# A two-layer hybrid trunk: later parameter loads and identity turns at the start, another order at the norm boundaries, in memory attention and in its projections

## What is computed

```python
for i in range(2):
    mem_kv = rmsnorm(mem, mem_norm[i]) @ w_mem_kv[i]              # keys and values of the memory
    proj = rmsnorm(h, norm_mix_pre[i]) @ w_in[i]
    y_mix = ssd_mixer(proj) if i == 0 else window_attention(proj)  # Mamba-2 SSD / 16 heads, window 128, sinks
    y_mem = memory_cross_attention(proj, mem_kv)                   # 4 heads of 128, softmax over 256 tokens
    h = h + rmsnorm(concat(y_mix, y_mem) @ w_out[i], norm_mix_post[i])
    f = square(relu(rmsnorm(h, norm_mlp_pre[i]) @ w_up[i])) @ w_down[i]   # 1024 -> 4096 -> 1024
    h = h + rmsnorm(f, norm_mlp_post[i])
```

## Time and profile before

| | us |
|---|---|
| median of 3 runs | 1384.0 (1383.21 to 1384.0) |
| profiled execution, own time | 1384.49 |
| its span, first to last instruction | 1382.4 |
| mean granted TensorE clock | 0.997 |
| TensorE busy with products and turns | 1346.0 (97%) |
| VectorE busy | 688.1 (50%) |
| ScalarE busy | 585.6 (42%) |
| GpSimd (POOL) busy | 121.3 (9%) |
| memory read | 133.44 MB, 99 GB/s over the span |

### The profile page before, as it was taken

How to read it: one execution, slowest core, us unless ns; L and a number is a source line. 1 busy time by engine, 2 the same in 40 slices (tenths; PEclk the granted TensorE clock), 3 DMA queues, 4 the chain that set the end, 5 groups by cost and what they waited for, 6 DMA issues and landing times.

```text
span 1382.4 us, 17791 instructions
## 1 busy us (share of the span) xinstructions
PE 1346.0 (97%) x6631; PEld 1114.8 (81%) x6631; DVE 688.1 (50%) x1070; ACT 585.6 (42%) x1103; POOL 121.3 (9%) x131
## 2 busy tenths in 40 slices
PE   6999999999999999999999999999999999999998
PEld 5788888888778888888888888776788888888886
DVE  5566686787435544223443454775364432244333
ACT  5555355566434443223432333664344432234321
POOL 0045252651000000000000000000000000000000
PEclk9999999999999999999999999999999999999999
DMA  6253433243422323242232133112223322322322
GB/s 205 72 144 94 118 100 113 99 147 105 164 92 63 110 87 107 97 133 91 91 107 92 62 99 111 47 62 77 70 67 98 97 96 99 114 92 92 106 92 77
DMA packets 75645, 137.73 MB, mean 100 GB/s; under 512 B 6391, under 2 KB 16951, under 8 KB 75575
## 3 DMA queue, kind: packets, MB, share of 16 engines
q1 hardware_dynamic: 71184, 134.76, 30.2%
q10 hardware_dynamic: 4390, 2.02, 0.8%
HBM read 133.44 MB, written 2.93 MB: 99 GB/s over the span
## 4 chain that ended last, share of the span: by engine, by line
PE 85%; DVE 8%; ACT 3%; issue 2%; DMA 1%; POOL 1%; ACTq 0%; DVEq 0%; SPq 0%; POOLq 0%
PE G L1656 56%; PE X L1656 12%; PE X L1679 5%; PE X L1727 3%; DVE conv L1209 2%; DVE wlo L1080 1%; PE X L1907 1%; PE X L1835 1%; PE X L2090 1%; PE G L1727 1%; ACT whi L555 1%; PE X L1826 1%; DMA raw<-in_w_up 1%; DVE ulo L1408 1%; PE X L2117 1%
## 5 line engine op out<-in xcount | busy, mean ns | idle before, releaser
L1080 DVE TENSOR_TENSOR wlo<-raw,whi 128x1024 fp32r<-128x1024 f32 x224 | 275.0, 1233 | 452.5 <-ACT whi L555 451.6
L555 ACT ACTIVATE whi<-raw 128x1024 fp32r<-128x1024 f32 x224 | 235.5, 1058 | 438.8 <-PE G L1656 234.0
L1656 PE MATMUL G<-uhi,whi 128*128 128x512 f32 x736 | 294.3, 400 | 3.1 <-DVE ulo L1097 1.8
L1656 PE MATMUL G<-uhi,wlo 128*128 128x512 f32 x736 | 287.1, 390 | 0.0
L1656 PE MATMUL G<-ulo,whi 128*128 128x512 f32 x736 | 286.6, 389 | 0.0
L1656 PEld LDWEIGHTS G<-uhi,whi 128*128 128x128 f32 x736 | 138.3, 188 | 33.2 <-issue 3.2
L1656 PEld LDWEIGHTS G<-uhi,wlo 128*128 128x128 f32 x736 | 138.1, 188 | 29.6
L1656 PEld LDWEIGHTS G<-ulo,whi 128*128 128x128 f32 x736 | 138.4, 188 | 28.4
L1656 PE MATMUL G<-whi,hidhi 128*128 128x512 f32 x256 | 99.6, 389 | 0.0
L1656 PE MATMUL G<-whi,hidlo 128*128 128x512 f32 x256 | 99.6, 389 | 0.0
L1656 PE MATMUL G<-wlo,hidhi 128*128 128x512 f32 x256 | 99.6, 389 | 0.0
(11 more groups left out here) (328 smaller groups left out, 2255.1 us busy)
## 6 DMA issues: line engine op xcount, KB each, us to landing
raw<-in_w_up SPq DMA_DIRECT2D x64, 512.0 KB, 3.8
raw<-in_w_down SPq DMA_DIRECT2D x64, 512.0 KB, 3.5
raw<-in_ssd_w_in SPq DMA_DIRECT2D x20, 512.0 KB, 3.6
raw<-in_w_mem_kv SPq DMA_DIRECT2D x16, 512.0 KB, 3.5
raw<-in_ssd_w_out SPq DMA_DIRECT2D x16, 512.0 KB, 3.5
raw<-in_swa_w_in SPq DMA_DIRECT2D x16, 512.0 KB, 3.8
raw<-in_ssd_w_in SPq DMA_DIRECT2D x16, 384.0 KB, 3.3
csrow<-cs_rows SPq DMA_DIRECT2D x16, 384.0 KB, 4.5
```

The lines of the kernel that those rows point to most:

```text
L555: act.activation(whi[q][:, :, :], raw[q % 2][:, :, :], ACT.Copy).then_inc(hi_done, 1)
L1080: dve.tensor_tensor(wlo[q][:, :, :], raw[q % 2][:, :, :], whi[q][:, :, :].bitcast(F32), ALU.subtract).then_inc(lo_done, 1)
L1656: mm = pe.matmul(o, st, mv, start=(kt == 0 and fresh and not go_on), stop=(q == total - 1 and k == 1), skip_group_check=True)
```

## The change

The rest of the code is as it was. Three of the eight parameter loads are gone, since nothing reads those rows of `par` (the gains come a second time through `g_post` and `g_pre`); `par` is filled accordingly (44 columns in place of 92).

```diff
+WARM = 20
-MEM_AT = {32 + 8 * i + r: (i, r) for i in range(2) for r in range(4)}
+MEM_AT = {29 + 11 * i + r: (i, r) for i in range(2) for r in range(4)}
-        g_gate = par[:, 80:92]
+        g_gate = par[:, 32:44]
@@ scalar: parameter loads
-            rows = (("mem_norm", 0, 16), ("norm_mix_pre", 16, 16), ("norm_mix_post", 32, 16),
-                    ("norm_mlp_pre", 48, 16), ("norm_mlp_post", 64, 16), ("ssd_gate_norm", 80, 12))
-            for name, r0, n in rows:
-                act.dma_start(par_rows[r0:r0 + n, 0, :],
+            for j, name in enumerate(("mem_norm", "norm_mix_pre")):
+                act.dma_start(par_rows[16 * j:16 * j + 16, 0, :],
                               a[name].rearrange("i (k p) -> (i k) p", p=P)).then_inc(par_in, 16)
-            act.dma_start(par_rows[0:80, 1, :],
-                          a["ssd_conv_w"][0].rearrange("w (k p) -> (w k) p", p=P)).then_inc(par_in, 16)
-            act.dma_start(par_rows[80:100, 1, :],
-                          a["ssd_conv_b"].rearrange("i (k p) -> (i k) p", p=P)).then_inc(par_in, 16)
...
             act.activation(eps[:, 4:5], eps[:, 0:1], ACT.Sqrt)
+            act.dma_start(par_rows[32:44, 0, :],
+                          a["ssd_gate_norm"].rearrange("i (k p) -> (i k) p", p=P)).then_inc(par_in, 16)
+            act.dma_start(par_rows[0:80, 1, :],
+                          a["ssd_conv_w"][0].rearrange("w (k p) -> (w k) p", p=P)).then_inc(par_in, 16)
+            act.dma_start(par_rows[80:100, 1, :],
+                          a["ssd_conv_b"].rearrange("i (k p) -> (i k) p", p=P)).then_inc(par_in, 16)
             for t in range(NT):
                 act.wait_ge(x_in[t], 16)
                 token_rms(t, x_tok[:, t, :], xn[:, t, :])
@@ scalar: mem_copy(i, j, part), part 0 banks 0 and 1 (or values of tile 0), part 1 the rest
                 if next_panel is not None:
+                    i, j = divmod(p // 4 - B_MEM, 2)
+                    if p % 4 == 3:
+                        mem_copy(i, j, 0)
                     ahead(*next_panel)
+                    if p % 4 == 3:
+                        mem_copy(i, j, 1)
...
-                else:
-                    mem_copy((blk - B_MEM) // 2, (blk - B_MEM) % 2)
@@ scalar: boundary
                 hi(nb, 1)
-                hi(nb, 2)
                 norm_out(m, 3)
                 norm_in(m, 2)
+                hi(nb, 2)
+                norm_in(m, 3)
                 hi(nb, 3)
-                norm_in(m, 3)
                 u_hi(m, 2)
                 u_hi(m, 3)
@@ vector: start
-            dve.wait_ge(par_tr, 2)
-            dve.tensor_copy(par[:, 0:92], X[3][:, 0:92]).then_inc(par_done, 1)
-            dve.tensor_scalar(par[:, 92:192], X[3][:, 128:228], 0.5, None, ALU.mult).then_inc(par_done, 1)
             for t in range(NT):
                 token_norm(t, x_tok[:, t, :], xn[:, t, :])
+                if t == 1:
+                    dve.wait_ge(par_tr, 2)
+                    dve.tensor_copy(par[:, 0:44], X[3][:, 3 * P:3 * P + 44]).then_inc(par_done, 1)
+                    dve.tensor_scalar(par[:, 92:192], X[2][:, 3 * P:3 * P + 100], 0.5, None,
+                                      ALU.mult).then_inc(par_done, 1)
@@ vector: memory_step
-                if tp == 0 and h >= 1:
+                if tp == 1 and h >= 1:
                     memory_lo(i, yh, yl, B, h - 1)
@@ vector: boundary
                 add_out(m, 3)
+                lo(nb, 2)
                 scaled(m, 2)
-                lo(nb, 2)
+                lo(nb, 3)
                 scaled(m, 3)
-                lo(nb, 3)
@@ vector: attention_panel
                         w_norm(u)
+                        if slot in Q_OUT:
+                            queries(N_QB, B_QB, 1, 2 * Q_OUT[slot])
                         if todo is not None:
                             ahead(*todo)
                             todo = None
...
-                    if slot in Q_OUT:
-                        queries(N_QB, B_QB, 1, 2 * Q_OUT[slot])
@@ tensor: split
-                            elif half == 0 and (q, b) == (3, 1):
+                            elif half == 0 and (q, b) == (3, 0):
                                 turn_u(m, 3, f)
@@ tensor: start
             pe.wait_ge(consts, 1)
-            pe.wait_ge(par_in, 128)
-            pe.transpose(X[3][:, 0:92], par_rows[0:92, 0, :], ident[0:92, 0:92]).then_inc(par_tr, 1)
-            pe.transpose(X[3][:, 128:228], par_rows[0:100, 1, :], ident[0:100, 0:100]).then_inc(par_tr, 1)
+            for x in range(WARM):
+                pe.transpose(G[0][:, 0:P], ident[:, :], ident[:, :])
             for t in range(NT):
+                if t == 1:
+                    pe.wait_ge(par_in, 80)
+                    pe.transpose(X[3][:, 3 * P:3 * P + 44], par_rows[0:44, 0, :], ident[0:44, 0:44]).then_inc(par_tr, 1)
+                    pe.transpose(X[2][:, 3 * P:3 * P + 100], par_rows[0:100, 1, :],
+                                 ident[0:100, 0:100]).then_inc(par_tr, 1)
                 pe.wait_ge(tok_norm, t + 1)
                 for k in range(KT):
-                    if t == 0 and k == KT - 1:
+                    if t == 1 and k == KT - 2:
                         pe.wait_ge(par_done, 2)
```

More of the change, by code:

```diff
@@ L580, in mem_hi, with mem_copy @@
                                    scale=g_mem[i][:, 2 * r + x:2 * r + x + 1]).then_inc(uhi_ready, 1)
-            def mem_copy(i, j):
+            def mem_copy(i, j, part):
                 n = 2 * i + j
                 if j == 0:
-                    for b in range(4):
+                    for b in (2 * part, 2 * part + 1):
                         group_ready(act, N_MEM + n, 4 * (B_MEM + n) + 4, b)
@@ L588, in mem_copy @@
                 else:
[L589 to L593, removed]
+                    t = part
+                    group_ready(act, N_MEM + n, 4 * (B_MEM + n) + 4, 2 * t + 1)
+                    for x in range(2):
+                        act.activation(memV[i][:, t, M * x:M * x + M], G[t][:, M * x:M * x + M],
+                                       ACT.Copy).then_inc(bank_free[t if x else 2 + t], 1)
             act.wait_ge(eps_done, 1)
             act.activation(eps[:, 4:5], eps[:, 0:1], ACT.Sqrt)
+            act.dma_start(par_rows[32:44, 0, :],
[4 more added lines that the diff above has]
+                          a["ssd_conv_b"].rearrange("i (k p) -> (i k) p", p=P)).then_inc(par_in, 16)
             for t in range(NT):
```

## The result

The changed kernel takes 1359.95 us (median of 6 runs, 1359.74 to 1360.34), the kernel before beside it 1383.08 (6 runs, 1381.85 to 1384.0): a ratio of 0.9833, with a 95% interval of 0.982 to 0.9845. The forecast was 1363.0. It had the sign right, and the mechanisms but for part of the start, and was 3 us too high; the result lies just under the low end of the range, 1360.0. The profiled execution took 1359.76 us (span 1357.7; before 1384.49 and 1382.4), so by its own time 24.7 us went where the sum had 21.0. By the medians it is 23.1: the profiled execution of the kernel before took 1.4 us more than its median, and that of the changed kernel 0.2 less.

What follows compares the result with a forecast made beforehand. TensorE was taken as the bound, busy 1346.0 of 1382.4 us, so only its waits could go. Terms 3.7 + 2.2 + 1.0 + 2.6 + 11.5 = 21.0 took 1384.0 (median) to 1363.0 us, range 1360 to 1369.

Steps and rivals of the forecast that it cites:

- The start: Up to the first product: fewer, reordered parameter loads and identity turns gain 4.2 or 3.1, middle 3.7 us.
- the 4.3 for no cover at all: At the start: the twenty identity turns cost nothing, but would cost 4.3 us if TensorE were needed meanwhile.
- Projections: Memory projections: earlier turns and copies ahead of the weight conversion remove waits, 0.6 + 1.6 = 2.2 us.
- Queries: Copy of `queries` on VectorE ahead of a weight conversion removes TensorE's wait, 1.0 us.
- Attention: Memory attention, second layer: `memory_lo` one step later removes waits of 3.5 us but 0.9, gain 2.6 us.
- Boundaries: Three norm boundaries: new order removes all waits and the low clock, 3.03 + 4.38 + 4.07 = 11.5 us.
- The margin of 0.5 us at tile 2's `u_tok`: Norm boundary: `scaled` for tile 2 ends at 446.1, its turns are due at 446.6, margin 0.5 us.
- The margin of 0.1 before the second half: Norm boundary: copy and subtraction after tile 3's turns need 2.0 us and have 2.1; last wait gone by 0.1.
- The stall moved: Rival at the norm boundaries: the stall moves instead of going, half of 11.5 us stays, 1368.7 us; chance 0.13.
- The low clock at the first products: Rival at the start: clock low at the first products, gain only 0.8 us, time 1365.9 us; chance 0.15.
- The parameters did not land late: Rival at the start: parameters land at 11 or 12 us, 2 us lost, time 1365 us; chance 0.05.
- No queue got a blocking wait: Rival in the state-space stretch: blocking waits in ScalarE's and VectorE's queues, eight places, 1387 us or more; chance 0.02.

Runs made afterwards that it cites:

- Experiments 4: Changed kernel with the copy of the queries put back behind the weight conversion; 1360.22 us.
- 11: Changed kernel with only VectorE's old order at the norm boundaries (scaled ahead of the weight's low part); 1362.59 us.
- 12: Changed kernel with 28 waits of TensorE on GpSimd added in two down projections of the first MLP; 1374.09 us.
- 5: Changed kernel with memory attention's subtraction (memory_lo) back at its earlier step, in both layers; 1361.89 us.
- 6: Changed kernel with the turns of the first memory set back in panels 32 to 35; 1359.94 us.
- 7: Changed kernel with all copies of a memory block back behind the weight conversion; 1361.04 us.
- 8: Changed kernel with tile 3's turns back behind the second bank of the fourth panel; 1361.14 us.
- 10: Changed kernel with forty turns of the identity at the start in place of twenty; 1360.09 us.
- experiment 3: Changed kernel without the twenty turns of the identity at the start; 1359.84 us.
- experiment 2: Kernel before, with 16 turns of the identity put in front of the third panel at each norm boundary; 1381.65 us.
- experiment 9: Changed kernel with a panel's low part on VectorE put behind the fourth normalisation of the second layer's memory attention; 1358.88 us.
- experiment 1: Changed kernel with the old order at the three norm boundaries (ScalarE, VectorE and the place of tile 3's turns); 1372.48 us.

## Why the prediction was wrong by 3 us

By the medians, 0.9 of the 3.05 us is the kernel before itself: the forecast starts from 1384.0, three runs, and six gave 1383.08. The rest is the change. The account below goes by the two profiled executions, 24.7 us for 21.0.

**The step that failed** is the pricing of a wait by the length that the profile lists. It stands in every term but the start, and it made each too small. "The first holds 3.03 of waiting and no clock drop, so the work itself is 8.0": from where the wait began to the second half it takes 7.38 us in the second and third boundary (6.79 from tile 2's turns at 792.43 to 799.22, and 0.59 for the six products ahead of them), so 0.6 us of the 8.0 were the overlaps and slow first products of the three waits. This makes 0.69 and 0.67 us of surplus in the two boundaries with the slow clock, 0.45 in the first, and likewise 0.32 in the projections, 0.28 in the queries and 0.44 in attention: 2.85 of the 3.7 us missing. (The listed waits themselves came out as the terms had them only in sum: 0.47 more in the projections, 0.30 less in the first boundary, 0.16 less in attention.) Experiments 4, 11 and 12 show it with waits between products: 0.29, 0.27 and 0.30 us per wait beyond its length. Where the wait stands before turns or a change of bank (5, 6, 7, 8) it was 0.13, 0.31, 0.09 and 0.15.

**The start** (3.7, measured 4.63) is the other term. Half of its 0.9 us is a choice: the sum gave 4.2 for turns at the faster pace and 3.1 for the slow one and took the middle, and they ran at the faster pace. The other half is the parameters. "three triggers (about 4.9, the first of them a slow one), then the first tile" counted the triggers behind the table load, one after the other; they ran beside it. ScalarE was ready 1.86 us before its first tile, and that tile still began at 5.10, near the forecast's 4.9, by luck: it now waited for x, which the forecast had landed by 4.6 and waited for nowhere. "The last of the five loads is triggered at about 4.4, as now, so I keep its landing at 9.63" was the step: triggered at 2.77 it took longer to land, 6.3 us for 5.22, but TensorE had the rows at 9.06. From there to the first product it took 5.73 us, and 6.1 by the forecast's middle. Tile 0's turns came at 7.62, for 7.4. The twenty turns end at 6.4 (6.2), before tile 0 is ready, and cost nothing that shows, as said. Twenty more, partly without cover, cost 1.0 us (10); the 4.3 for no cover at all was not tested, but it counted all of them at the slow pace and no wait behind them to absorb any. They bought less than the forecast assumed: it gave the loss of the clock at the first products 2.9 us, and without the turns it was at most 0.9 (3), because the turns of x raise the clock themselves by 11.9 us. So a good part of the start's reasoning on the clock bought nothing that the times can tell.

**Projections** (2.2, measured 2.99): the wait on `mlo` and the two on `memKT` went as worked out, the latter to 0.47 us ("`memKT` near 0.5"). A wait of 0.43 us on `csrow` further on, which the forecast did not price, went too; this is in part chance, as it comes and goes: of the twelve executions built on the changed kernel three lack it and nine show 0.18 to 0.31 us, and the kernel before with filled waits (2) shows 0.21. **Queries**: right but for the unlisted part. **Attention**: the wait left was to be 0.9 and is 1.06, with its cause as named: the weight conversion and the deferred subtraction ahead of the step after (940.65 and 941.80 in VectorE's timeline of experiment 9, where taking one of the two away removes it).

**Boundaries**: the work is on time, but closer than forecast. The margin of 0.5 us at tile 2's `u_tok` held every time, but in the changed kernel it was 0.3 (in the first boundary `scaled` runs from 437.26 to 438.54 and its turns start at 438.83). The forecast gave no margin for tile 3's row, and that is where TensorE stood: 0.30 us here and 0.15 in experiment 12, both at the first boundary, and not at all in the seven others of this order. The fourth panel, "ready at 447.6 for 449.7", was in time, but with some 0.3 us left and not 2.1 when its load came late, as above (low part done at 441.6, wanted at about 441.9), and tile 3's row behind it paid for that. The margin of 0.1 before the second half held every time.

**Rivals.** The stall moved only in small: 0.30 us at most, at the turns, as this rival had it. The low clock at the first products did not come in the changed kernel; it can come, though: in the execution of experiment 1, whose start is the changed kernel's, TensorE's timeline shows

```profile
7.14 0.66 PE L1827 MATMUL G<-ident,xn 128*128 128x128 f32 x4 [0.94 <-DVE xn L1097]
...
9.50 1.06 PE L1827 MATMUL G<-ident,xn 128*128 128x128 f32 x4
10.35 1.06 PE L1827 MATMUL X<-ident,xn 128*128 128x128 f32 x4
```

with the next four turns 0.5 us behind at 7.14 and 0.85 behind at 9.50, and the first product at 15.65: 1.1 us later than usual, not 2.9. The parameters did not land late: TensorE waited for them 0.9 us at most, with the rows by 9.1. No queue got a blocking wait. The rule of the Trainium skill that was weighed ("TensorE: Matmul & The Clock Gate", Part 4, PE-mode transpose: transposes do not engage the full clock) does not hold for these float32 turns: in experiment 3 nothing but turns ran before the pace doubled at 11.9, and in experiment 2 turns in the place of most of the wait kept the clock at 1.00 where it had gone to 0.50.

**The range** reached down by the bounds of the start, of attention and of the projections. The boundaries' upper bound was set at their forecast, 11.5, as though the listed waits were the most that could come back. They gave 13.0, and those 1.5 us carry the result past the low end.

## What to carry to other kernels

Price a wait of TensorE from the start of the instruction before it to the start of the one after it, less the usual pitch: in a stream of wide products that is the listed length plus about 0.3 us, so many short waits weigh far more than their sum in the list. Order a helper engine's queue so that what TensorE needs next stands in the pause in which that engine waits for another, and not behind it. And where a range is built from "all waits gone", leave room above it.

## What the hardware showed that was not expected

- A wait of TensorE listed as 0.22 us cost 0.52 between 512-column products (28 waits, 14.57 us).
- Triggers of loads on ScalarE's queue run while its table load is under way: three started at 1.81, 2.42 and 2.77 in a load from 1.74 to 3.02.
- The same wait does not always drop the clock: 1.94, 2.00 and 2.02 us left it at 2.4 GHz, 1.95, 2.10 and 2.20 were followed by 1.2 GHz. A drop cost 1.0 to 1.6 us.
- With the same code in front of it, the first product came anywhere from 14.29 to 14.79 us, once at 15.65 with the clock down. Single executions of this kernel can't be compared to better than about 1 us except by stages.
